# Third attention of an encoder layer: scores as one 96-row product per head, with odd heads and rotary strips moved to other partitions when they are copied

## What is computed

```python
def _apply_rope(x, ang):
    half = x.shape[-1] // 2
    x1, x2 = x[..., :half], x[..., half:]
    return jnp.concatenate([x1 * cos - x2 * sin, x2 * cos + x1 * sin], axis=-1)

def _mla_attention(cq, ckv, ckr, pos, q_norm_g, w_uq, kv_norm_g, w_ukv):
    q = (_rms_norm(cq, q_norm_g) @ w_uq).reshape(b, s, 8, 64 + 32)
    kv = (_rms_norm(ckv, kv_norm_g) @ w_ukv).reshape(b, s, 8, 64 + 64)
    q_rope = _apply_rope(q[..., 64:], ang[:, :, None, :])
    k_rope = _apply_rope(ckr, ang)
        sc = (jnp.einsum('bqhd,bkhd->bhqk', qn, k_nope)
              + jnp.einsum('bqhr,bkr->bhqk', qr, k_rope)) * 96 ** -0.5
        p = jax.nn.softmax(sc, axis=-1)
        return jnp.einsum('bhqk,bkhd->bqhd', p, v)
```

## Time and profile before

| | us |
|---|---|
| three runs | 1649.14, 1650.2, 1651.13; median 1650.2 |
| the profiled execution, own time | 1651.03 |
| its span, first to last instruction | 1649.1 |
| PE, DVE, ACT, POOL busy | 1334.7 (81%), 509.6 (31%), 241.1 (15%), 33.5 (2%) |
| mean granted TensorE clock | 0.912 of full speed |
| transfers | 504.41 MB, 306 GB/s over the span |

### The profile page before, as it was taken

How to read it: one execution, slowest core, us unless ns; L and a number is a source line. 1 busy time by engine, 2 the same in 40 slices (tenths; PEclk the granted TensorE clock), 3 DMA queues, 4 the chain that set the end, 5 groups by cost and what they waited for, 6 DMA issues and landing times.

```text
span 1649.1 us, 18201 instructions
## 1 busy us (share of the span) xinstructions
PE 1334.7 (81%) x7594; PEld 793.4 (48%) x7594; DVE 509.6 (31%) x1007; ACT 241.1 (15%) x585; POOL 33.5 (2%) x46
## 2 busy tenths in 40 slices
PE   8999999999666566767699999999995665656655
PEld 7886688755122122233168757886642121312211
DVE  4235464444211212221112462643531211211121
ACT  2214410032010000000021244000410000000001
POOL 2000000001000000000000000000100000000000
PEclk9999999999888778788899999999998887888788
DMA  9933245259999999999995423533899999999996
GB/s 299 327 115 116 77 132 217 102 230 386 413 422 421 421 409 422 421 422 420 419 345 186 121 85 94 198 135 114 328 365 423 421 421 422 420 421 421 421 421 281
DMA packets 141719, 504.41 MB, mean 306 GB/s; under 512 B 9152, under 2 KB 82944, under 8 KB 93504
## 3 DMA queue, kind: packets, MB, share of 16 engines
q1 hardware_dynamic: 137920, 494.41, 76.9%
q0 software_dynamic: 1824, 4.56, 1.0%
q10 hardware_dynamic: 1888, 4.19, 0.7%
HBM read 502.08 MB, written 1.05 MB: 305 GB/s over the span
## 4 chain that ended last, share of the span: by engine, by line
PE 55%; DMA 38%; SPq 2%; DVE 2%; issue 1%; ACT 1%; DVEq 0%; ACTq 0%
DMA ring<-in_w_dram 38%; PE banks L1668 25%; PE banks L1914 6%; PE banks L1974 5%; PE banks L1674 4%; PE banks L2069 3%; SPq L562 2%; PE banks L1816 1%; PE banks L1826 1%; PE banks L1847 1%; PE banks L1868 1%; PE banks L2104 1%; PE banks L2055 1%; PE banks L1726 1%; PE banks L1811 1%
## 5 line engine op out<-in xcount | busy, mean ns | idle before, releaser
L1914 PE MATMUL banks<-ring,v 128*32 128x512 f32 x1920 | 293.0, 751 | 182.5 <-DMA ring<-in_w_dram 175.1
L1668 PE MATMUL banks<-hT,ring 128*128 128x256 f32 x1440 | 317.6, 380 | 0.5 <-ACT kx_wide L821 0.5
L1668 PEld LDWEIGHTS banks<-hT,ring 128*128 128x128 f32 x1440 | 272.0, 190 | 43.1 <-issue 5.0
L1914 PEld LDWEIGHTS banks<-ring,v 128*32 128x32 f32 x1920 | 79.0, 133 | 383.5 <-issue 381.1
L1974 PE MATMUL banks<-ring,probT 128*32 128x512 f32 x960 | 143.9, 723 | 89.8 <-DMA ring<-in_w_dram 84.3
L1974 PEld LDWEIGHTS banks<-ring,probT 128*32 128x32 f32 x960 | 38.2, 129 | 178.7 <-issue 168.2
L1343 DVE COPY q<-banks 128x512 f32<-128x512 f32 x16 | 11.1, 692 | 245.4 <-PE banks L1974 214.5
L1868 PE MATMUL banks<-v,h 128*128 128x128 f32 x512 | 65.8, 289 | 13.5 <-issue 13.2
L1339 DVE TENSOR_TENSOR q<-banks,q 128x512 f32<-128x512 f32 x16 | 11.1, 692 | 212.1 <-PE banks L1914 212.1
L1868 PEld LDWEIGHTS banks<-v,h 128*128 128x128 f32 x512 | 62.4, 202 | 28.0 <-issue 28.0
L1674 PE MATMUL banks<-ring,hT 128*128 128x256 f32 x256 | 57.2, 381 | 0.0
(11 more groups left out here) (312 smaller groups left out, 1286.8 us busy)
## 6 DMA issues: line engine op xcount, KB each, us to landing
ring<-in_w_dram SPq DMA_DIRECT2D x360, 1024.0 KB, 19.2
ring<-in_w_in_dram SPq DMA_DIRECT2D x52, 1024.0 KB, 11.0
ring<-in_w_branch_dram SPq DMA_DIRECT2D x8, 1024.0 KB, 5.1
ring<-in_w_out_dram SPq DMA_DIRECT2D x8, 1024.0 KB, 5.9
ring<-in_w_branch_dram SPq DMA_DIRECT2D x8, 512.0 KB, 3.4
k<-in_w_dram SPq DMA_DIRECT2D x4, 1024.0 KB, 8.5
shared<-in_w_dram SPq DMA_DIRECT2D x4, 1024.0 KB, 12.2
ring<-in_w_dram SPq DMA_DIRECT2D x8, 512.0 KB, 20.7
```

Source lines behind the costliest of these rows:

```text
L1668: last = nc.tensor.matmul(dst, w[:, k, cols], src[:, k, :], start=k == 0, stop=k == kn - 1)
L1914: last = nc.tensor.matmul(bank[2 + m][e * CAP:(e + 1) * CAP, :], xt[:, k, e * CAP:(e + 1) * CAP], ws[e](r), start=k == 0, stop=k == KD - 1)
```

## The change

- **Scores.** Queries and keys of the third attention now lie with one head per tile on partitions 0 to 95: 64 plain rows and 32 rotary rows. A unit's scores are two 96-row products in place of four.
- **Copies of cq0, cq1, ck0, ck1.** ScalarE copies the even heads (partitions 0 to 63), VectorE the odd ones, from partitions 64 to 127 to 0 to 63. Both have the job in step 11, 12, 13 or 14, and who needs it waits for both.
- **Rotary queries.** cqr's copy goes to another tile (`qr`). rope() ends after its two multiplications; the addition for the queries is then four additions of 32 partitions x 512 elements, each from its strip to partitions 64 to 95. That of the key is one addition, to partitions 64 to 95 of head 0's tile.
- **Rotary key to all heads.** GpSimd copies it from there to the other seven tiles (32 partitions x 1792 elements), after `kr`; the first unit of the third attention waits for it.
- **Constants.** The three matrices of rotation lie in another order and another buffer, and their load waits until the first job of the layer has freed its slot. That is the value for which the next load of the list waits too.

```diff
@@ -92,7 +92,7 @@
-    c[:, C_TURN:] = np.concatenate([same, swap, swap * strip], axis=1)
+    c[:, C_TURN:] = np.concatenate([swap * strip, same, swap], axis=1)
@@ -150,8 +150,8 @@
-         ("cq0", 15, 0, "act"), ("cqr", 15, 1, "act"), ("cq1", 16, 1, "act"),
-         ("ck0", 17, 0, "act"), ("cr", None, 0, "dve"), ("ck1", 17, 0, "dve"),
+         ("cq0", 15, 0, "act+dve"), ("cqr", 15, 1, "act"), ("cq1", 16, 1, "act+dve"),
+         ("ck0", 17, 0, "act+dve"), ("cr", None, 0, "dve"), ("ck1", 17, 0, "act+dve"),
@@ -250,7 +250,8 @@
-        turn_mats = k0[:, :, :].rearrange("p a n -> p (a n)")[:, 5 * SEQ:5 * SEQ + 3 * P]
+        turn_mats = h[:, 1, SEQ:SEQ + 3 * P]
+        qr = wide[:, 0:2, :]
@@ -370,7 +371,7 @@
-        N_COPIED = {e: sum(j[3] == e for j in JOBS) for e in ("act", "dve")}
+        N_COPIED = {e: sum(e in j[3] for j in JOBS) for e in ("act", "dve")}
@@ -383,8 +384,8 @@
-            e = JOBS[n][3]
-            eng.wait_ge(copied[e], l * N_COPIED[e] + count_before(lambda j: j[3] == e, n))
+            for e in JOBS[n][3].split("+"):
+                eng.wait_ge(copied[e], l * N_COPIED[e] + count_before(lambda j: e in j[3], n))
@@ -541,6 +542,7 @@
+                        wait_free(sp, l, 0)
@@ -669,6 +671,10 @@
+                wait_copied(pool, l, "kr")
+                plain(pool)
+                r = slice(C_NOPE, C_DH)
+                nc.gpsimd.tensor_copy(kc[r, 1:8, :], kc[r, 0:1, :].broadcast_to([C_ROPE, 7, SEQ])).then_inc(setup_pool, 1)
@@ -805,12 +811,15 @@
+                elif name == "cqr":
+                    act.wait_ge(ca_rstd, 2 * l + 1)
+                    last = nc.scalar.activation(qr, b2, ACT.Copy, scale=C_DH ** -0.5)
                 elif kind == "cq":
-                    c = 4 if i == "r" else 2 * int(i)
-                    last = nc.scalar.activation(q0[:, c:c + 2, :], b2, ACT.Copy, scale=C_DH ** -0.5)
+                    c = 4 * int(i)
+                    last = nc.scalar.activation(q0[0:C_NOPE, c:c + 4:2, :], b2[0:C_NOPE], ACT.Copy, scale=C_DH ** -0.5)
                 elif kind == "ck":
-                    c = 2 * int(i)
-                    last = nc.scalar.activation(kc[:, c:c + 2, :], b2, ACT.Copy)
+                    c = 4 * int(i)
+                    last = nc.scalar.activation(kc[0:C_NOPE, c:c + 4:2, :], b2[0:C_NOPE], ACT.Copy)
@@ -909,7 +918,7 @@
-                        if JOBS[JOB_NAMES.index(name)][3] == "act":
+                        if "act" in JOBS[JOB_NAMES.index(name)][3]:
@@ -1195,15 +1205,15 @@
-            def rope(l, n, dst, plain_src, turned_src, groups):
+            def rope(l, n, plain_dst, plain_src, turned_src, groups):
...
-                tmp = oBC[:, 6:6 + groups, :]
+                tmp = oBC[:, 8 - groups:8, :]
                 nc.vector.tensor_tensor(tmp, turned_src, sin, ALU.mult).then_inc(rope_step, 1)
-                nc.vector.tensor_tensor(dst, plain_src, cos, ALU.mult).then_inc(rope_step, 1)
+                nc.vector.tensor_tensor(plain_dst, plain_src, cos, ALU.mult).then_inc(rope_step, 1)
                 dve.wait_ge(rope_step, l * 4 + (2 * n + 2))
-                return nc.vector.tensor_tensor(dst, dst, tmp, ALU.add)
+                return tmp
@@ -1228,15 +1238,22 @@
-                    last = rope(l, 0, kc[:, 4:5, :], b2[:, 0:1, :], b2[:, 1:2, :], 1)
+                    tmp = rope(l, 0, oBC[:, 6:7, :], b2[:, 0:1, :], b2[:, 1:2, :], 1)
+                    last = nc.vector.tensor_tensor(kc[r, 0, :], oBC[r, 6, :], tmp[r, 0, :], ALU.add)
                 elif kind == "ck":
-                    c = 2 * int(i)
-                    last = nc.vector.tensor_copy(kc[:, c:c + 2, :], b2)
+                    c = 4 * int(i) + 1
+                    last = nc.vector.tensor_copy(kc[0:C_NOPE, c:c + 3:2, :], b2[C_NOPE:])
+                elif kind == "cq" and name != "cqr":
+                    c = 4 * int(i) + 1
+                    last = nc.vector.tensor_scalar(q0[0:C_NOPE, c:c + 3:2, :], b2[C_NOPE:], C_DH ** -0.5, None, ALU.mult)
...
-                    last = rope(l, 1, q0[:, 4:6, :], q0[:, 4:6, :], b2, 2)
+                    tmp = rope(l, 1, qr, qr, b2, 2)
+                    for strip in range(4):
+                        rows, hd = slice(C_ROPE * strip, C_ROPE * strip + C_ROPE), 2 * (strip % 2) + strip // 2
+                        last = nc.vector.tensor_tensor(q0[r, hd:hd + 5:4, :], qr[rows], tmp[rows], ALU.add)
@@ -1403,7 +1420,7 @@
-                        if JOBS[JOB_NAMES.index(name)][3] == "dve":
+                        if "dve" in JOBS[JOB_NAMES.index(name)][3]:
@@ -1510,7 +1527,7 @@
-                dve.wait_ge(setup_pool, 2 * l + 3)
+                dve.wait_ge(setup_pool, 3 * l + 4)
@@ -1703,7 +1720,7 @@
-                        last = nc.tensor.matmul(b[:, c * SEQ:(c + 1) * SEQ], turn_mats[:, c * P:(c + 1) * P], kr_parts,
+                        last = nc.tensor.matmul(b[:, c * SEQ:(c + 1) * SEQ], turn_mats[:, (c + 1) * P:(c + 2) * P], kr_parts,
@@ -1741,7 +1758,7 @@
-                    last = nc.tensor.matmul(b[:, :], turn_mats[:, 2 * P:3 * P], q0[:, 4:6, :], start=True, stop=True)
+                    last = nc.tensor.matmul(b[:, :], turn_mats[:, 0:P], qr, start=True, stop=True)
@@ -1795,6 +1812,8 @@
+                if i == C0:
+                    pe.wait_ge(setup_pool, 3 * l + 2)
@@ -1803,12 +1822,8 @@
-                        rows = slice(64 * j, 64 * j + 64)
-                        nc.tensor.matmul(dst[:, j, :], q0[rows, u - 8, qs], kc[rows, u - 8, :], start=True, stop=False)
-                    for j in range(2):
-                        group, at = divmod(u - 8, 2)
-                        rows = slice(64 * j + C_ROPE * at, 64 * j + C_ROPE * at + C_ROPE)
-                        last = nc.tensor.matmul(dst[:, j, :], q0[rows, 4 + group, qs], kc[rows, 4, :], start=False, stop=True)
+                        hd = 2 * (u - 8) + j
+                        last = nc.tensor.matmul(dst[:, j, :], q0[0:C_DH, hd, qs], kc[0:C_DH, hd, :], start=True, stop=True)
@@ -2136,7 +2151,7 @@
-                pe.wait_ge(setup_pool, 2 * l + 3)
+                pe.wait_ge(setup_pool, 3 * l + 4)
```

## The result

Six runs of each kernel: before 1649.14 to 1651.37 us, median 1650.44; changed 1656.55 to 1663.42 us, median 1658.56. The ratio is 1.0054 (95% interval 1.0044 to 1.0064), and the medians lie 8.1 us or 0.49% apart: slower, where 1654.0 us and 0.23% (3.8 us) had been forecast. Two things are to be explained: the size, and that the changed kernel's runs spread over 6.9 us and those of before over 2.2 (over 3.3 and 3.8 in later comparisons of 25 and 23 runs).

The account below looks back on a forecast made before the run. TensorE bounds the attention, transfers the experts, and delays in the mixing block shift the end. 2.0 + 2.5 - 2.6 = +1.9 us a layer, +3.8 in all, gives a median of 1654.0 us; range 1648.5 to 1659.0.

Parts of the forecast that it names:

- the two waits: TensorE idle ahead of `cs` for VectorE, 2.0 us a layer, and ahead of unit 13's transposes for ScalarE, 2.5 us.
- rival 2: GpSimd's key copy runs at the two-input rate, 4.5 us: delay 4.2, +4.1 a layer, 1658.4 us; chance 0.17.
- the forecast's own range: 1651.2 us (delay 0.9, wait 2.2, gain 2.6) to 1656.6 us (delay 2.7, wait 2.6, gain 2.1).
- rival 4: The 96-row score products save nothing, 0.63 us each: 2.0 + 2.5 a layer, 1659.2 us; chance 0.05.
- GpSimd's lock: GpSimd's key copy holds VectorE's L1412, for which TensorE waits ahead of `cs`: 2.0 us a layer.
- The estimate of 2.7 us: Length of GpSimd's 1792-element key copy, estimated from 769 ns for 512 elements; a delay of 2.2 to 2.7 us.
- The wait at unit 13's transposes: Four additions for `cr` delay ScalarE's copy of unit 12's transposes, so TensorE waits at `turn_probs(13)`: 2.5 us a layer.
- the 2.16 in that sum: Extra VectorE time for `cr`'s four additions if none overlaps the next: 4 x 0.69 - 0.60 us.
- The scores: Third attention: two 96-row products in place of four save 0.37 us a unit, 2.6 us a layer.
- ck0's, cq0's and cq1's extra copies: Odd heads' copies on VectorE, some 0.69 us each for cq0 and cq1, hidden in idle time or done early: no cost.

Follow-up runs that it names:

- filled waits: Changed kernel, with TensorE filling its idle time ahead of `cs` and of unit 13's transposes with thrown-away products: 1654.65 us, ratio 1.0025.
- the second profile: The changed kernel once more, unaltered, for another profiled execution: 1655.42 us, beside 1651.66 for the kernel before.
- the short and the long copy: Changed kernel with GpSimd copying the rotary key to three tiles (1654.88 us), against the changed kernel's own copy to seven (1658.56 us).
- the kernel with the old four products: Changed kernel with GpSimd's copy behind the foldings and the four additions later, scores again four products a unit on the new layout: 1677.25 us, ratio 1.0153.
- the best kernel: Changed kernel with GpSimd's copy behind the foldings and the four query additions placed later: 1646.66 us, ratio 0.9978.

## Why the prediction missed

**The step that failed is the pricing of the two waits by their length alone.** The sum, 2.0 + 2.5 - 2.6 = +1.9 a layer, has no term for TensorE's clock behind them. Without a fall a layer is 1.04 to 1.10 us slower (filled waits; the second profile's layer one). Each fall adds up to 1.64 behind one of four waits: three times in the first profile, once in the second. The prediction spoke of the clock only in rival 2, for a wait of 5 us. It showed 1.00 beside small gaps and 0.70 on average with 5 us idle of 8, had no row between, and left that open ground out of the sum and of the forecast's own range, which ends at 1656.6.

By the medians the 8.1 us are 2.1 that the blocks cost without the clock, 3.9 that filling the waits took away (1658.56 - 1654.65), and 2.1 that no run explains.

**What was luck.** 1658.56 us is nearly rival 2's number, 1658.4, but not by its mechanism: it had the copy at 4.5 us and the delay at 4.2, and they were 1.5 to 2.1 and 1.47. Nor by that of rival 4 (1659.2), since the scores did save time. The wide range, 1648.5 to 1659.0, holds the result only because it was stretched for these two.

**The terms it had**, with what they measured:
- GpSimd's lock: right in place and engine. 2.21 - 0.74 = 1.47 us for 2.0. The copy ran at 0.83 to 0.93 ns an element, not 1.3. By the rule that whoever issues first has the port, from the Trainium skill (SBUF — State Buffer, "Who interferes with whom"), L1410 goes first; the rows of the short and the long copy agree: L1410 (L1427 now) keeps its 0.69 us, and L1412 (L1429 now) doesn't keep its 0.42. The estimate of 2.7 us from the Trainium skill (GPSIMD Engine Reference, section 3.1) was far off: the row of the copy alone is 1.67. The same section of the Trainium skill has 1.03 cycles an element for the simplest bodies, from which I estimate 0.86 ns, and the trace agrees.
- The wait at unit 13's transposes: right in place, order and size, 2.63 us for 2.5. The additions didn't overlap (0.70 us each), as the 2.16 in that sum had it.
- The scores: the stretch with the last 5 units took 47.13 us before (176.88 to 224.01) and takes 45.52 now (182.76 to 228.28), with 0.58 more of waiting inside, so 2.19 / 5 = 0.44 us a unit for 0.37. Over 8 units, less the 0.58 lost at step 20, that is 2.9 a layer for 2.6.
- ck0's, cq0's and cq1's extra copies, and the constants' load: nothing, as said. From `cs` to `cr`'s product TensorE took 24.91 us before (135.64 to 160.55) and 26.55 now (137.06 to 163.61), 1.64 more, which is the fall.

These give 1.47 + 2.63 - 2.9 = +1.2 a layer, below the forecast's 1.9 and near the 1.04 to 1.10 measured; what the profiled blocks have above that is the clock.

**One reading was wrong.** The prediction set aside the Trainium skill's rule (TensorE: Matmul & The Clock Gate, Part 3) that two products on different rows take the time of one, because the pair took 0.63 and a full product 0.44. The kernel with the old four products shows that one such product alone takes 0.625 us between products of another layout, so a pair does take the time of one and the rule agrees with the runs. What made the pair dear is argued from rows and not isolated by a run. In the kernel before, two pairs of one layout stand one behind the other between full products and take 1.07 us together:

```profile
62.27 1.13 PE L1816 MATMUL banks<-k,q 64*128 64x256 f32 x8
63.34 7.17 PE L1674 MATMUL banks<-ring,hT 128*128 128x256 f32 x32
```

One of them adds 0.44, the time of a full product, and the other 0.63. So some 0.19 us seems to go with each change of layout. The 96-row products hardly pay it: the two at 181.89 take 0.87 us to the next start, and two full ones 0.89. The change then saves by having fewer changes of layout, which also fits that what stands beside a unit got 0.1 shorter (cv0 from 1.83 to 1.72 us, start to start, at full clock).

**What stays open.** The blocks explain 2.1 us of the filled kernel's +4.3, and have -4.8 where the best kernel's median has -3.7. Some 0.6 of either gap is that the profiled execution of before stood 0.6 above its median. The rest lies outside the mixing blocks, where the stretches of single profiles lie between 1.3 us below and 1.5 above those of before, and no run isolated it. Nor do the falls explain the slowest runs: four (6.6 us) and the blocks' 2.1 end at 1659.1 us, and two of the changed kernel's six took 1661.74 and 1663.42. The filled kernel, with no fall in its profile, still spread over 3.4 us.

## What to carry to other kernels

Price a wait on TensorE not by its length alone: behind idle times of 2.2 and 2.6 us its clock was at half here, in some executions and not in others. Runs that spread far wider than before are a reason to look at the granted clock behind each wait, though not a proof. A few products into a bank that is overwritten anyway took that part away; moving the late work (here four additions, ck1's copy and GpSimd's; none by more than three steps) took most of both away. When a copy is moved to another engine, look for the small instruction that it can hold up, and ask who waits for that one.

## What the runs showed of the hardware

- TensorE's clock was at 1.2 GHz for some 3 us behind idle times of 2.21 and 2.63 us in four of eight such places over two profiles of one kernel (nine of sixteen over six profiles of four kernels), and at 2.4 GHz in the others and behind 1.36 and 1.88 us.
- Four products of 256 columns that alternate between 64 and 32 rows took 2.50 us, 0.625 each; two of 96 rows 0.87 to 0.97. Two pairs of 64 rows one behind the other took 1.07 us, one alone 0.63. That a change of layout costs some 0.19 us is worked out from these.
- GpSimd's copy of float32 within SBUF took 0.83 ns more for each element more (1.23 us for 768, 2.08 for 1792), and a VectorE addition with two SBUF inputs that started under it ended 0.28 us after it (1.78 us for 0.42).
- VectorE's instructions on 32 or 64 partitions took as long as those on 128 (0.69 to 0.70 us for 512 elements), also those that move to other partitions.
